# A chunked state-space scan on one Trainium2 core: state products taken in halves between the other products, two multiplications handed from GpSimd to ScalarE

## The reference

```python
def ssd_scan(x, dt, a, bm, cm, s0, chunk):
    ...
    cs = jnp.cumsum(dt * a.reshape(G, HG).astype(f32), axis=2)
    seg = cs[:, :, :, None] - cs[:, :, None, :]
    decay = jnp.exp(jnp.where(mask, seg, -jnp.inf))
    xdt = x * dt[..., None]
    cb = jnp.einsum('bcign,bcjgn->bcijg', cm, bm)
    y_diag = jnp.einsum('bcijg,bcijgh,bcjghp->bcighp', cb, decay, xdt)
    decay_end = jnp.exp(cs[:, :, -1:] - cs)
    st = jnp.einsum('bcjgn,bcjgh,bcjghp->bcghpn', bm, decay_end, xdt)
    chunk_decay = jnp.exp(cs[:, :, -1])
    ...                                  # state: s * dec + st, chunk after chunk
    y_off = jnp.einsum('bcign,bcghpn,bcigh->bcighp', cm, s_start, jnp.exp(cs))
    y = (y_diag + y_off).reshape(B, T, H, P)
...
    y = y + d_skip[:, None] * xs
    y = gated_group_rmsnorm(y.reshape(B, T, D_INNER), z, ssm_norm_w)   # (y * silu(z)), norm over a group, * w
    merged = jax.nn.sigmoid(g_att) * att + jax.nn.sigmoid(g_ssm) * y
```

## Time and profile before

| | before |
|---|---|
| time, median of 3 runs | 2505.29 us (2500.51 to 2505.69) |
| time of the profiled execution | 2508.58 us |
| its span | 2506.8 us |
| PE busy | 2245.6 us, 90% |
| DVE busy | 1473.1 us, 59% |
| POOL busy | 835.7 us, 33% |
| ACT busy | 611.0 us, 24% |
| first transpose of the first chunk, first score product of attention | 930.7 us, 1168.6 us |

### The profile page before, as it was taken

The page is one execution under the profiler, slowest core; times in us unless marked ns, Lnnn a source line. Parts: engine busy times, 40 slices in busy tenths (PEclk is TensorE's granted clock), DMA queues, the critical chain, the costliest instruction groups (busy, mean ns, idle before and its releaser), DMA issues.

```text
span 2506.8 us, 33911 instructions
## 1 busy us (share of the span) xinstructions
PE 2245.6 (90%) x13159; PEld 2010.0 (80%) x13159; DVE 1473.1 (59%) x2413; ACT 611.0 (24%) x1009; POOL 835.7 (33%) x728
## 2 busy tenths in 40 slices
PE   7897999999999957774889998789999999999995
PEld 4893469999999946663677873279999999999994
DVE  1733425899999966775899855336423233233237
ACT  2202320110013332223667751112110010110103
POOL 0220024333333325332565531341423324234235
PEclk9898999999999978886999997889999999999997
DMA  6113412222222131333321015432111101101022
GB/s 255 65 57 120 151 67 101 94 93 88 95 92 92 67 104 50 85 84 77 68 51 26 26 36 192 159 135 85 50 35 33 67 33 50 50 33 67 33 87 82
DMA packets 110371, 203.21 MB, mean 81 GB/s; under 512 B 10405, under 2 KB 78005, under 8 KB 98741
## 3 DMA queue, kind: packets, MB, share of 16 engines
q1 hardware_dynamic: 94610, 163.90, 20.3%
q10 hardware_dynamic: 15670, 38.19, 3.9%
HBM read 161.06 MB, written 41.13 MB: 81 GB/s over the span
## 4 chain that ended last, share of the span: by engine, by line
PE 40%; DVE 5%; POOL 3%; issue 2%; DMA 2%; ACT 2%; SPq 1%; DVEq 0%; POOLq 0%; ACTq 0%
PE pj L1899 31%; PE px L1325 3%; PE pj L1314 2%; PE pj L1558 1%; DVE Pr L1449 1%; ACT PT L1378 1%; DMA raw<-in_w_out 1%; POOL q_hl L1248 1%; DMA St<-in_state_ssm 1%; DVE m8b L1435 0%; POOL wlo L1856 0%; PE pj L1302 0%; SPq L1477 0%; DVE M L1412 0%; PE pj L1301 0%
## 5 line engine op out<-in xcount | busy, mean ns | idle before, releaser
L240 PE MATMUL pj<-act_hi,whi 128*128 128x344 f32 x1344 | 431.7, 321 | 3.5 <-POOL wlo L223 2.4
L240 PE MATMUL pj<-act_hi,wlo 128*128 128x344 f32 x1344 | 430.6, 320 | 0.0
L240 PE MATMUL pj<-act_lo,whi 128*128 128x344 f32 x1344 | 430.3, 320 | 0.0
L215 POOL CAST whi<-raw 128x512 fp32r<-128x512 f32 (+2 forms) x100 | 66.8, 693 | 631.3 <-PE pj L240 403.2
L1899 PE MATMUL pj<-ahi,whi 128*128 128x344 f32 x816 | 263.0, 322 | 10.7 <-DVE alo L2055 8.7
L1899 PE MATMUL pj<-ahi,wlo 128*128 128x344 f32 x816 | 261.3, 320 | 0.0
L1899 PE MATMUL pj<-alo,whi 128*128 128x344 f32 x816 | 260.8, 320 | 0.0
L240 PEld LDWEIGHTS pj<-act_hi,whi 128*128 128x128 f32 x1344 | 253.9, 189 | 3.8 <-issue 2.6
L240 PEld LDWEIGHTS pj<-act_hi,wlo 128*128 128x128 f32 x1344 | 253.8, 189 | 0.0
L240 PEld LDWEIGHTS pj<-act_lo,whi 128*128 128x128 f32 x1344 | 253.4, 189 | 0.0
L1899 PE MATMUL pj<-u_lo,d_hi 128*128 128x344 f32 x720 | 230.7, 320 | 0.0
(11 more groups left out here) (376 smaller groups left out, 4592.7 us busy)
## 6 DMA issues: line engine op xcount, KB each, us to landing
raw<-in_w_in SPq DMA_DIRECT2D x29, 1024.0 KB, 4.8
raw<-in_w_ada SPq DMA_DIRECT2D x24, 1024.0 KB, 4.8
raw<-in_w_up SPq DMA_DIRECT2D x16, 1024.0 KB, 4.9
raw<-in_w_down SPq DMA_DIRECT2D x16, 1024.0 KB, 4.8
scr_g<-O ACTq DMA_DIRECT2D x16, 516.0 KB, 2.7
scr_c<-E ACTq DMA_DIRECT2D x16, 516.0 KB, 2.7
xb<-scr_c SPq DMA_DIRECT2D x8, 1024.0 KB, 6.4
qt<-scr_q SPq DMA_DIRECT2D x32, 256.0 KB, 5.3
```

The costliest lines, as they stand in the source:

```text
L215: ins = pool.tensor_copy(whi[:, hs, 0:kt, c0:c1], a)
L240: ins = pe.matmul(pj[:, hs, n, 0:W3], w[:, hs, k], a[:, k, c], start=(k == 0 and m == 0), stop=(k == kt - 1 and m == 2))
```

## The change

Three things are changed, all in the SSD stage. On PE, the four matmuls of C with the state are issued two by two behind the inner values of the first and of the second group, and the four matmuls to the state stand behind those of the third group and ahead of those of the fourth. On DVE, each half of the state's part of yn is made as soon as its two matmuls are there, between the ML; the decay of the state moves ahead of the wait for the inner values, and the new state moves ahead of the skip sum. The skip term and the weighted gate are made by ACT instead of POOL, in 16 instructions of one block of 128x128 with a scale for each partition, behind the root and ahead of the squares.

```diff
--- before.py
+++ after.py
@@ -971,6 +971,24 @@
                 if j == 1:
                     ins.then_inc(SD["ss"], 1)
 
+            def from_state(s, j):
+
+                for g in (2 * j, 2 * j + 1):
+                    ins = pe.matmul(pjf[0][:, g * 256:g * 256 + 256], xb[:, s, 12 + g], ST[:, g * 256:g * 256 + 256],
+                                    start=True, stop=True)
+                ins.then_inc(SD["yo"], 1)
+
+            def to_state(at, later):
+
+                pe.wait_ge(SD["xw"], at(1, 1))
+                pe.wait_ge(SD["ex"], at(1, 1))
+                if later:
+                    pe.wait_ge(SD["rt"], at(1, 0))
+                for g in range(4):
+                    ins = pe.matmul(pxf[:, g * 256:g * 256 + 256], Bn[:, g], xw[:, 4 * g:4 * g + 4].rearrange("p h d -> p (h d)"),
+                                    start=True, stop=True)
+                ins.then_inc(SD["dst"], 1)
+
             def chunk(at, s, i, first, later):
 
                 pe.wait_ge(s_cin[s], i * 48 + 48)
@@ -1017,20 +1035,10 @@
                             ins = pe.matmul(pjf[1][:, hh * 64:hh * 64 + 64], ML[:, (g - 1) % 2, h], xdt[:, hh],
                                             start=True, stop=True)
                         ins.then_inc(SD["y"], 1)
-
-                for g in range(4):
-                    ins = pe.matmul(pjf[0][:, g * 256:g * 256 + 256], xb[:, s, 12 + g], ST[:, g * 256:g * 256 + 256],
-                                    start=True, stop=True)
-                ins.then_inc(SD["yo"], 1)
-
-                pe.wait_ge(SD["xw"], at(1, 1))
-                pe.wait_ge(SD["ex"], at(1, 1))
-                if later:
-                    pe.wait_ge(SD["rt"], at(1, 0))
-                for g in range(4):
-                    ins = pe.matmul(pxf[:, g * 256:g * 256 + 256], Bn[:, g], xw[:, 4 * g:4 * g + 4].rearrange("p h d -> p (h d)"),
-                                    start=True, stop=True)
-                ins.then_inc(SD["dst"], 1)
+                    if g in (1, 2):
+                        from_state(s, g - 1)
+                    if g == 3:
+                        to_state(at, later)
 
                 pe.wait_ge(SD["yn"], at(1, 1))
                 for m in range(KT):
@@ -1070,6 +1078,13 @@
                                    ).then_inc(SD["decay"], 1)
                 if later:
                     root(at, first)
+                act.wait_ge(s_cin[s], i * 48 + 48)
+                for m in range(KT):
+                    ins = act.activation(xD[:, m], xb[:, s, m], ACT.Copy, scale=dskip[:, m:m + 1])
+                ins.then_inc(SD["xd"], 1)
+                for m in range(KT):
+                    ins = act.activation(gc[:, s, m], gc[:, s, m], ACT.Copy, scale=par[:, 72 + m:73 + m])
+                ins.then_inc(SD["gcw"], 1)
                 act.wait_ge(SD["g"], at(1, 1))
                 act.activation(xD[:], gg[:, s], ACT.Square).then_inc(SD["sq"], 1)
 
@@ -1096,13 +1111,6 @@
                 pool.wait_ge(SD["ex"], at(1, 1))
                 pool.tensor_tensor(xw[:], xdt[:], ex[:, 16:32].unsqueeze(2).broadcast_to([P, 16, 64]), ALU.mult
                                    ).then_inc(SD["xw"], 1)
-                pool.wait_ge(s_cin[s], i * 48 + 48)
-                if later:
-                    pool.wait_ge(SD["ss"], at(1, 0))
-                pool.tensor_tensor(xD[:], xb[:, s, 0:KT], dskip[:].unsqueeze(2).broadcast_to([P, KT, P]), ALU.mult
-                                   ).then_inc(SD["xd"], 1)
-                pool.tensor_tensor(gc[:, s], gc[:, s], par[:, 72:80].unsqueeze(2).broadcast_to([P, KT, P]), ALU.mult
-                                   ).then_inc(SD["gcw"], 1)
 
             chunks(pool, chunk)
 
@@ -1159,24 +1167,26 @@
                         norm(at, s, bass.ds(i * 256 + (s - 2) * P, P))
                     if g == 2 and later:
                         gate(at, 1 - s)
+                    if g in (1, 2):
+                        j = g - 1
+                        dve.wait_ge(SD["yo"], at(2, g))
+                        if g == 1 and later:
+                            dve.wait_ge(SD["yt"], at(1, 0))
+                        link(dve.tensor_tensor(in_blocks(yn, j), by_head(pjf[0], j),
+                                               ex[:, 8 * j:8 * j + 8].rearrange("p (u a) -> p u a", u=2).unsqueeze(3).broadcast_to([P, 2, 4, 64]),
+                                               ALU.mult))
 
                 steps(1 - s, bass.ds(i * 2 + (s + 1), 1))
-                dve.wait_ge(SD["yo"], at(1, 1))
+                st3 = ST.rearrange("p (h d) -> p h d", d=64)
+                link(dve.tensor_tensor(st3, st3, ex[:, 32:48].unsqueeze(2).broadcast_to([P, 16, 64]), ALU.mult))
                 dve.wait_ge(SD["y"], at(4, 4))
-                for j in range(2):
-                    ins = dve.tensor_tensor(in_blocks(yn, j), by_head(pjf[0], j),
-                                            ex[:, 8 * j:8 * j + 8].rearrange("p (u a) -> p u a", u=2).unsqueeze(3).broadcast_to([P, 2, 4, 64]),
-                                            ALU.mult)
-                    link(ins)
                 link(dve.tensor_tensor(in_blocks(yn, 0), in_blocks(yn, 0), by_head(pjf[1], 0), ALU.add))
                 dve.tensor_tensor(in_blocks(yn, 1), in_blocks(yn, 1), by_head(pjf[1], 1), ALU.add).then_inc(SD["yn"], 1)
-                st3 = ST.rearrange("p (h d) -> p h d", d=64)
-                link(dve.tensor_tensor(st3, st3, ex[:, 32:48].unsqueeze(2).broadcast_to([P, 16, 64]), ALU.mult))
+                dve.wait_ge(SD["dst"], at(1, 1))
+                dve.tensor_tensor(ST, ST, pxf, ALU.add).then_inc(SD["st"], 1)
                 dve.wait_ge(SD["yt"], at(1, 1))
                 dve.wait_ge(SD["xd"], at(1, 1))
                 dve.tensor_tensor(gg[:, s], pjf[0][:, 0:D].rearrange("p (k t) -> p k t", k=KT), xD, ALU.add).then_inc(SD["yr"], 1)
-                dve.wait_ge(SD["dst"], at(1, 1))
-                dve.tensor_tensor(ST, ST, pxf, ALU.add).then_inc(SD["st"], 1)
                 dve.wait_ge(SD["yr"], at(1, 1))
                 dve.tensor_tensor(gg[:, s], gg[:, s], zc[:, s], ALU.mult).then_inc(SD["g"], 1)
 
```

## The result

The changed kernel takes 2494.43 us (median of 7 runs, 2490.36 to 2501.19), the kernel before, measured beside it, 2505.29 (7 runs, 2500.51 to 2507.57). The ratio is 0.9962, 95% interval 0.995 to 0.9973: faster by 10.9 us, where the forecast was 36.8 and its range ended at 2484.

The account below looks back on a forecast made before the run. No engine was full: each chunk was one chain of waits. First chunk -2.2, second -4.4, six others -29.3 and z -1.0 made -36.9 us, forecast 2468.5, range 2461 to 2484.

Parts of the forecast that it names:

- Sum: SSD stage: first chunk 22.1 us, second 22.1, six others 136.1 for 165.4; with z, 36.9 us less in all.
- The state product in halves: PE's product from the state: 0.95 us a half at 2.4 GHz; chain without loads 22.1 us a chunk.
- -1.0 for z: DVE's product with z directly behind the skip sum: another 1.0 us off the stage's end.
- A low clock at each chunk's start: Rival, chance 0.20: PE idles for loads, starts at 0.50; +2.0 us in five or six chunks, +11, so 2479.
- Slower: Rival, chance 0.04: clock low through the whole chunk; six chunks of 31 us for 27.7, +20, so 2525.
- the writes of M: DVE, with POOL's two multiplications gone: two writes fall from 4.72 to 1.45 us, 0.68 each.
- 16 instructions on ACT: Skip term and weighted gate on ACT behind the root: 4.8 us, between 4.8 and 6.2, costing the path nothing.
- PE's wait for the root: New wait ahead of the product to the state, which precedes the last inner values: some 1.5 us.
- the loads as the next bound: Loads hang on the gate's end, landing 10.5 us later at S+22.8 (S: chunk's first transpose); steady chunks 22.8 us.

Follow-up runs that it names:

- the clock held: Changed kernel plus 15 unused products of constants a chunk at three PE waits: 0.9857 of before. Old order with skip and gate on ACT plus 9 such products: 0.9839.
- the loads out of the way: Kernels with unused products of constants, PE waiting at a chunk's start only for xb's load: new order 0.9832, old order 0.9849, new with the root's product last 0.9779.
- the first filled run: Changed kernel plus 15 unused products of constants a chunk, ahead of the product to the state and on both sides of the yn transposes: 2471.56 us, 0.9857 of before.

## Why the prediction was wrong

**The step that failed is "Sum", with "The state product in halves" under it:** both priced the whole chain at 2.4 GHz. The third to the eighth chunk take 160.3 us (978.1 to 1138.4) for the forecast's 136.1, the second 25.6 for 22.1, the first 21.5 for 22.1: the forecast is 27.1 us too short, which is the whole gap between -36.9 and what arrived (from the first start to the last skip sum's end 207.4 us for 216.2, so -8.8, and -1.0 for z). In the seventh chunk the excess over 22.1 is 5.4 us: 3.3 up to the first ML (S+8.2 for S+4.9), 1.3 in the product to the state (3.23 for 1.89), 0.35 in the last inner values (1.45 for 1.1), 0.4 in small links. With the clock held, the same order gave -36.7.

**The rival "A low clock at each chunk's start"** had the mechanism, at 0.20, but its condition was wrong, and its price too low for most chunks. I let it depend on a wait for the load; five of the eight starts had none, only 1.57 and 1.4 us of idleness around the yn transposes. And I priced 2.6 us of path, or 2.0 us a chunk, as if the clock came back in the middle of seg. In the fifth and sixth chunk, the two behind the first that did wait for the load, that is about right (first ML at S+7.1 and S+6.3, for S+4.7 with the clock held). In the third, fourth, seventh and eighth it stayed down over the transposes, C·B, the sums and the seg products of the first two groups, and the first ML came at S+8.2. The second low stretch, behind the root's wait that I had drawn myself, had no price at all. "Slower", a low clock through the chunk, went too far: the clock was at 1.00 between 1093 and 1102.

**Right, by their rows:** the writes of M (691 ns each, 0.68 forecast); 16 instructions on ACT (2.43 us for eight, 4.9 in all; forecast 4.8), at no cost to the path; halves of 1.08 us (0.95), for which DVE waits 1.8 us in all, in three places; PE's wait for the root, 1.73 us (1.5); and the loads as the next bound at 22.8, as soon as the clock is held.

**What the parts were worth** I had not asked. Moving skip and gate to ACT is 34 us alone by its ratio, the new order alone 12; on top of the ACT part the order costs 18 us by the length and 25 by the ratios. That cost goes with the clock: with the clock held the two orders are about equal (208.7 for the new one, 207.0 for the old, and the intervals of the ratios overlap). Putting the root's product last, which takes one of the new waits out of PE's queue, gives part of it back. The order pays only with the clock held and the loads out of the way: 202.2 against 207.0 of length as it was drawn, where the ratios' intervals overlap, and 191.8 with the root's product last.

**Still open:** why the kernel before started its chunks at 1.00 behind 1.23 and 1.46 us of idleness, while 1.57 and 1.4 led to 0.50 here. The idleness alone doesn't decide: with the ACT part alone, 1.47 us were followed by 0.50 and 1.70 by 1.00, and with the product to the state last, 2.56 by 0.50 and 3.74 by 1.00. Why the clock came back sooner in the fifth and sixth chunk than in the others is open too.

## What to carry to other kernels

When a change removes TensorE's waiting in a stage that waits anyway, price the new chain at both clocks; a chunk's first 5 us of path at 0.50 can eat what the reordering gained. A few products of constants at the waits are a cheap test: if the time falls, the clock was the cost; if it doesn't, look in the trace for the wait that took its place, as in the kernel before. And run each half of a change alone: one half can carry the gain and the other hide it.

## What was unexpected of the hardware

- TensorE stayed at 0.50 for some 8 us while it was busy without a break (1085 to almost 1093 in the windows above), yet in the same kernel's sixth chunk (1058.71) it was back some 3.5 us behind a start at 0.50, with the same work. The Trainium skill (TensorE: Matmul & The Clock Gate, "HAM oscillation") tells of groups that start at the low clock each time because each waits for a transfer. The trace agrees on the pattern, but most of these waits were for VectorE.
- More work made the kernel faster: 15 products that nobody reads, 3.9 us of TensorE a chunk, took 26 us off (0.9962 to 0.9857 of before; 26.4 of the length).
- Eight scaled copies of 128x128 on ACT, each 389 ns long, took 2.43 us together, so one starts some 0.29 us behind the other.
- An earlier stage, untouched by all edits, ran at 0.83 between 320 and 340 in the profile of before and at 1.00 in that of the first filled run; the SSD stage then began 6.1 us earlier (924.6 against 930.7). A profile's span can shift by that with no edit in sight, so a stage is better compared by its own length.
